# MLA softmax three items ahead of its transposes; state-space rows as one product, two buffers of decayed x, first merges later

## What is computed

```python
def block(args):                                   # MLA, 16 heads, blocks of 128 queries
    s = einsum('bqhd,bkhd->bhqk', qn, k_nope) + einsum('bqhr,bkr->bhqk', qr, k_rope)
    s = where(key_pos <= q_pos, s * scale, -inf)
    p = softmax(s, axis=-1)
    return einsum('bhqk,bkhv->bqhv', p, v)

def ssd_scan(xh, dt, a, bmat, cmat):               # chunks of 128, 4 groups of 8 heads
    x = xh * dt
    a_cum = cumsum(dt * a, axis=2)
    decay = exp(where(tri, a_cum[:, :, :, None] - a_cum[:, :, None, :], -inf))
    cb = einsum("bclgn,bcsgn->bclsg", cm, bm)
    y_diag = einsum("bclsgr,bcsgrp->bclgrp", cb[..., None] * decay, x)
    decay_states = exp(a_cum[:, :, -1:] - a_cum)
    states = einsum("bclgn,bclgrp->bcgrpn", bm, x * decay_states[..., None])
    # scan over chunks: h = h * exp(a_cum[:, :, -1]) + states
    y_off = einsum("bclgn,bcgrpn->bclgrp", cm, prev) * exp(a_cum)[..., None]
    return y_diag + y_off

merged = sigmoid(g_att) * y_att + sigmoid(g_ssm) * y_ssm
```

## Time and profile before

| | us |
|---|---|
| median of 3 runs | 2668.32 |
| lowest, highest | 2663.45, 2671.43 |
| profiled execution, device time | 2666.76 |
| its span in the profile | 2664.9 |
| TensorE busy in the span | 2557.8 (96%) |
| VectorE busy | 1531.3 (57%) |
| GpSimd busy | 1138.1 (43%) |
| ScalarE busy | 670.0 (25%) |
| mean granted TensorE clock | 0.988 |

### The profile page before, as it was taken

How to read it: one execution, slowest core, us unless ns; L and a number is a source line. 1 busy time by engine, 2 the same in 40 slices (tenths; PEclk the granted TensorE clock), 3 DMA queues, 4 the chain that set the end, 5 groups by cost and what they waited for, 6 DMA issues and landing times.

```text
span 2664.9 us, 31050 instructions
## 1 busy us (share of the span) xinstructions
PE 2557.8 (96%) x11716; PEld 2035.1 (76%) x11716; DVE 1531.3 (57%) x2061; ACT 670.0 (25%) x1315; POOL 1138.1 (43%) x765
## 2 busy tenths in 40 slices
PE   8999999999988999999999999999989998999998
PEld 6888888888766778888886677777766666788886
DVE  4764665464776533735556674444445787677721
ACT  2003520021444421201113213333322442222200
POOL 4333455555522135555553353333322224555554
PEclk9999999999999999999998999999999999999999
DMA  6334556665522236665664474454454435565665
GB/s 206 125 111 128 165 190 193 199 192 189 174 79 77 67 111 190 193 197 194 206 190 142 137 239 158 158 170 141 150 199 133 148 115 166 183 196 190 190 194 169
DMA packets 149562, 436.63 MB, mean 164 GB/s; under 512 B 14064, under 2 KB 18352, under 8 KB 149424
## 3 DMA queue, kind: packets, MB, share of 16 engines
q1 hardware_dynamic: 64480, 200.29, 25.6%
q0 software_dynamic: 67840, 201.35, 21.7%
q10 hardware_dynamic: 17104, 33.14, 3.6%
HBM read 417.90 MB, written 16.83 MB: 163 GB/s over the span
## 4 chain that ended last, share of the span: by engine, by line
PE 50%; POOL 18%; issue 17%; DVE 9%; DMA 2%; DVEq 2%; ACT 1%; POOLq 0%; ACTq 0%; SPq 0%
POOL w_lo L422 15%; PE bank L479 12%; PE bank L481 12%; PE bank L482 12%; POOL w_hi L394 4%; DMA projections<-spill_out 1%; PE bank L1127 1%; PE bank L1118 1%; DVE mla_probs L2188 1%; PE bank L950 1%; PE bank L684 1%; PE bank L937 1%; DVE rope_sum L2106 1%; DVE mla_probs L2405 1%; PE bank L1153 1%
## 5 line engine op out<-in xcount | busy, mean ns | idle before, releaser
L422 POOL TENSOR_TENSOR w_lo<-w_raw,w_hi 128x1024 fp32r<-128x1024 f32 x375 | 901.9, 2405 | 11.7 <-DMA w_hi<-stream 3.7
L394 POOL DMA_DIRECT2D w_hi<-stream x376 | 227.6, 605 | 1497.4 <-PE bank L479 1297.9
L479 PE MATMUL bank<-x_hi,w_hi 128*128 128x512 f32 x1464 | 588.3, 402 | 17.8 <-POOL w_lo L408 11.5
L481 PE MATMUL bank<-x_lo,w_hi 128*128 128x512 f32 x1464 | 573.7, 392 | 0.0
L482 PE MATMUL bank<-x_hi,w_lo 128*128 128x512 f32 x1464 | 573.4, 392 | 0.0
L479 PEld LDWEIGHTS bank<-x_hi,w_hi 128*128 128x128 f32 x1464 | 277.2, 189 | 101.2 <-issue 39.8
L482 PEld LDWEIGHTS bank<-x_hi,w_lo 128*128 128x128 f32 x1464 | 277.1, 189 | 59.0
L481 PEld LDWEIGHTS bank<-x_lo,w_hi 128*128 128x128 f32 x1464 | 277.4, 189 | 56.7 <-issue 2.5
L2053 DVE TENSOR_TENSOR relu_sq<-relu 128x512 f32<-128x512 f32 x64 | 181.8, 2840 | 97.7 <-ACT relu L1428 97.7
L479 PE MATMUL bank<-hidden_hi,w_hi 128*128 128x512 f32 x512 | 199.2, 389 | 0.0
L481 PE MATMUL bank<-hidden_lo,w_hi 128*128 128x512 f32 x512 | 199.2, 389 | 0.0
(11 more groups left out here) (441 smaller groups left out, 4536.1 us busy)
## 6 DMA issues: line engine op xcount, KB each, us to landing
w_hi<-stream POOLq DMA_DIRECT2D x376, 512.0 KB, 4.8
w_raw<-stream SPq DMA_DIRECT2D x376, 512.0 KB, 3.7
projections<-spill_out ACTq DMA_DIRECT2D x56, 256.0 KB, 2.1
ssm_x<-projections ACTq DMA_DIRECT2D x4, 1024.0 KB, 6.8
gate_tiles<-projections ACTq DMA_DIRECT2D x16, 256.0 KB, 2.9
ssm_z<-projections ACTq DMA_DIRECT2D x16, 256.0 KB, 2.6
residual<-x_in SPq DMA_DIRECT2D x4, 512.0 KB, 6.8
toeplitz_hi<-toeplitz_rows_hi POOLq DMA_DIRECT2D x4, 512.0 KB, 6.4
```

The lines of the kernel that those rows point to most:

```text
L394: e.dma_start(in_slot(whi, t % SLOTS, o), in_stream(o)).then_inc(hi_ready[t % SLOTS], 16)
L422: e.tensor_tensor(wlo[:, s, :], raw[:, s, :], whi[:, s, :].bitcast(F32), ALU.subtract).then_inc(lo_ready, 1)
L479: mm = e.matmul(out, wh, rh, start=first, stop=False)
L481: e.matmul(out, wh, rl, start=False, stop=False)
```

## The change

Four things change. In MLA the distance of 2 becomes `MLA_AHEAD = 3` in the loops of TensorE, ScalarE and VectorE; `mpr` keeps its three buffers, and the conditions of the waits stay. The high and low rows of the cumulative sums become one tile of 64 partitions (`sat_rows`), selected by a column of two identities above each other (`both`, which ScalarE writes in two copies), so that `rows` and `decay_rows` take one matmul where they took two. `ssm_xd` gets a second buffer: VectorE makes the first two decayed x at B and the third after S0. And VectorE merges a0, a1 and a2 after T3, S0 and S2 instead of T0, T3 and S1.

```diff
+MLA_AHEAD = 3
...
-        sah, sal = at("ssm_acum_t_hi", 198, [32, S], F32R), at("ssm_acum_t_lo", 202, [32, S], F32R)
+        sat_rows, both = at("ssm_acum_t", 198, [64, S], F32R), at("hi_and_lo_row", 207.5625, [64, 32], F32R)
+        sah, sal = sat_rows[0:32, :], sat_rows[32:64, :]
...
-        sxd, sbn = at("ssm_xd", 148, [P, S]), ...
+        sxd, sbn = [at(f"ssm_xd{x}", kb, [P, S]) for x, kb in enumerate((148, 202))], ...
...
-                for n in range(MLA_ITEMS + 2):
+                for n in range(MLA_ITEMS + MLA_AHEAD):
                     if n < MLA_ITEMS:
                         scores(n)
-                    m = n - 2
+                    m = n - MLA_AHEAD
...
-                        sel = identr[0:32, 2 * n + q:2 * n + q + 1].broadcast_to([32, P])
-                        e.matmul(o[:, :], sel, sah[:, :], start=True, stop=False)
-                        e.matmul(o[:, :], sel, sal[:, :], start=False, stop=False)
+                        sel = both[:, 2 * n + q:2 * n + q + 1].broadcast_to([64, P])
+                        e.matmul(o[:, :], sel, sat_rows[:, :], start=True, stop=False)
...
-                    e.matmul(bank[3][:, :], sel, sah[:, :], start=True, stop=False)
-                    e.matmul(bank[3][:, :], sel, sal[:, :], start=False, stop=True).then_inc(ea_full, 1)
+                    e.matmul(bank[3][:, :], sel, sat_rows[:, :], start=True, stop=True).then_inc(ea_full, 1)
...
-                    if n >= 6 and (n - 6) % 4 == 0:
-                        out_low((n - 6) // 4)
+                    done = n - MLA_AHEAD - 4
+                    if done >= 0 and done % 4 == 0:
+                        out_low(done // 4)
...
                     elif kind == "B":
                         decayed_x(g, 0)
+                        decayed_x(g, 1)
...
-                        if c < 2:
-                            decayed_x(g, c + 1)
+                        if c == 0:
+                            decayed_x(g, 2)
...
                 def decayed_x(g, c):
-                    e.drain()
+                    if c == 0:
+                        e.drain()
+                    if 3 * g + c >= 2:
+                        e.wait_ge(st_pe, 3 * g + c - 1)
...
-                    units("first", i)
+                    units("first", {3: 0, 5: 3, 7: 6}.get(i, -1))
```

More of the change, by code:

```diff
@@ L344, in build @@
         sst = [at(f"ssm_state{x}", 136 + 6 * x, [P, 3, S]) for x in range(2)]
-        sxd, sbn = at("ssm_xd", 148, [P, S]), [at(f"ssm_b_nat{x}", 150 + 2 * x, [P, ST, P]) for x in range(2)]
+        sxd, sbn = [at(f"ssm_xd{x}", kb, [P, S]) for x, kb in enumerate((148, 202))], [at(f"ssm_b_nat{x}", 150 + 2 * x, [P, ST, P]) for x in range(2)]
         sgt = [[at(f"ssm_g{p}{q}", 164 + 4 * p + 2 * q, [P, S]) for q in range(2)] for p in range(2)]
@@ L600, in build @@
         STEP_UNITS = []
-        for _s in range(MLA_ITEMS + 2):
+        for _s in range(MLA_ITEMS + MLA_AHEAD):
             _now = []
@@ L1230, in prep @@
                             e.wait_ge(e_bn, g + 1)
-                        e.matmul(bank[4][:, :], sbn[g % 2][:, c, :], sxd[:, :], start=True, stop=True).then_inc(st_pe, 1)
+                        e.matmul(bank[4][:, :], sbn[g % 2][:, c, :], sxd[(3 * g + c) % 2][:, :], start=True, stop=True).then_inc(st_pe, 1)
                 for i, task in enumerate(PREP):
@@ L1631, in projections @@
                         e.wait_ge(dt_pe, 1)
-                        e.activation(sah[:, :], bank[2][0:32, :], ACT.Copy).then_inc(dt_act, 1)
+                        for x in range(2):
+                            rows_ = slice(32 * x, 32 * x + 32)
+                            e.activation(both[rows_, :], identr[rows_, rows_].bitcast(F32), ACT.Copy)
+                        e.activation(sah, bank[2][0:32, :], ACT.Copy).then_inc(dt_act, 1)
             def sparse_attention():
@@ L1705, in exponentials @@
                         e.activation(ssel[:, :, :],
-                                     identr[0:32, 2 * n:2 * n + 8].bitcast(F32).unsqueeze(2).broadcast_to([32, 8, 64]), ACT.Copy)
+                                     both[:, 2 * n:2 * n + 8].bitcast(F32).unsqueeze(2).broadcast_to([64, 8, 64]), ACT.Copy)
                     e.wait_ge(sg_sel, n + 1)
@@ L2321, in time_sums @@
                 e.tensor_copy(sat[:, :, :], bank[1][:, 0:P].rearrange("p (c n) -> p c n", n=32))
-                tt(sal[:, :], bank[2][0:32, :], sah[:, :].bitcast(F32), ALU.subtract)
+                tt(sal, bank[2][0:32, :], sah.bitcast(F32), ALU.subtract)
                 e.drain()
```

4 lines of the change are left out of this document (2 added, 2 removed).

## The result

The changed kernel takes 2651.41 us (median of 7 runs, 2648.74 to 2655.71), the kernel before on the same chip 2671.43 (7 runs, 2662.40 to 2674.72). The ratio is 0.9935, 95% interval 0.9920 to 0.9951: 17.4 us faster by it (13 to 21 in the interval), 20.0 by the medians. The prediction had 32 us, and its range ended at 2649. The profiled execution's span is 2649.7 us against 2664.9.

What follows compares the result with a forecast made beforehand. The prediction took TensorE to bound both stages. MLA's 14.6 us and the state space's 17.6 summed to 32.2 us off the profiled execution's 2666.76, giving 2634.6, or 2636 as median; range 2625 to 2649.

Steps and rivals of the forecast that it cites:

- The 17.2 us of waits go: MLA: twelve waits of TensorE's transposes for VectorE's scaled probabilities, 17.2 us in all, disappear with one more item of distance.
- Nine ordinary heads pay 0.2 each: MLA: in nine heads the output product newly waits 0.2 us for ScalarE's copy, 1.8 us in all.
- Three rotary heads pay 1.2 each: MLA: in three heads with VectorE's rotary steps between, the output product waits 1.2 us each, 3.6 in all.
- an output product that waits over 1 us in a head with units: MLA: named beforehand as a sign that the prediction would be wrong.
- 4.0 us of clock back: MLA: of 8.6 us lost to TensorE's low clock, 4.0 are regained, bounds 0 and 5.
- Unit-less heads, period about 8.9, no gain: MLA: two heads without units take about 8.9 us between output products, 8.97 before; waits of 0.9 return, 1.8 in all.
- The tail, 10.25 to 8.9: MLA's end: from the last but one output product to the first product of `mla_o`, 10.25 us becomes 8.9.
- The first items: MLA's first six items stay bound by VectorE's rotary steps; the first output product comes some 0.7 us later.
- State space, start, 7.5 us: State-space start: unit a1 4.8 us earlier, clock 1.3, first state product's wait 0.6 and second's 0.8 less; 7.5 in all.
- 48 matmuls at 0.23: State-space head steps: 48 removed matmuls are worth 0.23 us each, 11.0 us, bounds 8 and 15.8.
- 0.9 us lost to waits: Head steps: longer waits for chunk copies take 1.2 us, the last state products' waits give 0.3; 11.0 becomes 10.1.
- The chain in all heads: Rival: each of 15 MLA heads pays 0.9 us or more, MLA gives 3 us, the whole 2648; chance 0.12.

Runs made afterwards that it cites:

- e5: The changed kernel with GpSimd's `w_lo` of three weight tiles filled with zeros instead of computed, leaving out part of four units; 2638.08 us, ratio 0.9884 to before.
- e2: The changed kernel with `MLA_AHEAD` back at 2, so only the state-space edits; 2655.80 us, ratio 0.9953 to the kernel before.
- e1: The kernel before with `MLA_AHEAD = 3` and its three uses, nothing else; 2666.05 us, ratio 0.9992 to the kernel before.
- e18: The changed kernel with MLA distance back at 2 and twelve `w_lo` held by waits for VectorE's scalings; 2637.38 us, ratio 0.9891 to before.
- e20: e18 with VectorE's state of the next group ahead of the merge in the p = 3 head steps; 2642.08 us, ratio 0.9888 to before.
- e9: The changed kernel with VectorE's state of the next group ahead of the merge in the p = 3 head steps; 2650.37 us, ratio 0.9932 to before.

## Why the prediction was wrong, point by point

**The 17.2 us of waits go**: right, 1.5 are left, under the 5 named. The scalings held by `w_lo` that it expected to stay are gone too: none in MLA lasts over 0.6 us after. **Nine ordinary heads pay 0.2 each**: they pay nothing.

**Three rotary heads pay 1.2 each: this is the step that failed.** They paid 3.5. Without the meeting of `w_lo` and `rope_sum` it is 0.85 (e5), so the order on ScalarE and VectorE was read rightly and GpSimd left out. The prediction named this as a sign of being wrong (an output product that waits over 1 us in a head with units), without a cause for it. The trace of before had it: a scaling held 2.83 us by `w_lo`, and a `rope_sum` only 0.7 us ahead of the next `w_lo`. I kept VectorE's durations and moved only TensorE. But the start of `w_lo` hangs on TensorE (it follows the first product out of a tile, 1.5 us behind it before and 1.4 after), and taking 1.8 us of waiting and the half clock behind it out of TensorE moved it 2.35 us against VectorE. 3 x 2.3 = 6.9 us of the missing 10.9.

**4.0 us of clock back**: nothing came back (0.95 over MLA after, 0.96 before; 0.98 or more was named), since each 3.5 us wait had its own low clock behind it. Counted as the prediction does, 10.2 us are lost to the clock against 8.5: the 4.0 and 1.7 more. With the 6.9, and less the 1.8 that the ordinary heads don't pay, this makes 10.8 of the 10.9. It follows from the same step: in e5 no low clock stands behind the three output products (6.0 us lost, at the first items and the tail).

**Unit-less heads, period about 8.9, no gain**: 8.8 measured; their product waits 0.4 and not 0.9. **The tail, 10.25 to 8.9**: 9.0. **The first items**: the first output product comes 1.2 us later, 0.7 predicted.

**State space, start, 7.5 us**: 6.0 in the profiled execution, 7.7 in e2, which has no low clock there. Piece by piece: a1 5.1 (4.8 predicted), chunks 1.44 apart (1.5), the first state product's wait down by 0.45 (0.6), the second's by 0.75 (0.8). Right.

**48 matmuls at 0.23**: right, three to a step make 0.70 in steps without waits. **0.9 us lost to waits**: mis-sized. Up to the last rows 45 of the matmuls are gone, 10.35 us, and e2, without a low clock, gains 8.4 (185.25 to 176.8): 1.9 lost. The transposes' waits for chunk copies grew by 1.8 (1.2 predicted); I had not listed the wait of `ssm_head_rows`' product for VectorE's `ssm_y`, which has its bank (1.1 us in two places, none before); the last state products' waits fell by 0.9 (0.3 predicted). In the last step that product waits another 1.4, and from its rows to the product that sums the squares of y it is 0.8 longer than before (19.7 us in e2 against 18.9), where 0.7 less was counted on: 3.4 lost of the 11.0 in all. In the profiled execution of after another 1.6 is clock.

**The rivals.** The chain in all heads (MLA 3 us, 2648) is near in time and wrong in mechanism: e1's and the full kernel's heads with units don't wait unless they are rotary. The measured 3.7 us of MLA has another cause.

The prediction drew on the Trainium skill (TensorEngine Tiling (Array Packing), Tiling Modes, Key Properties), which says that a change of the tiling mode drains TensorE. The runs agree as far as the time goes: it is 0.43 and 0.43 us between 64-row and 128-row products, and a removed matmul was worth 0.23 and not 0.33. That the added time is a drain no run here shows.

## What to carry to other kernels

When a wait of the bounding engine is taken away, everything that this engine releases (slots, and so the loads and conversions of a helper engine) starts earlier against the other engines: look at what runs on the third engine within the removed time, on both sides, and whether the two can hold each other. The work of an engine that is rarely waited for can be placed by a wait of its own, and here nine such waits were worth more (12 us by the ratio, 7 to 17 in its interval) than another item of distance (2, 0 to 5); the place has a latest point too, the next reader of what it makes. Cutting its work into pieces without a gap between them made both kernels slower here. And a stage of one profiled execution can differ by 4 us from another of the same code by the clock alone (e18 and e20): compare waits first.

## What was not expected of the hardware

VectorE got no turn between four GpSimd instructions that followed each other directly, 0.70 us apart: `rope_sum` took 4.87 us beside 2.81 of them. A GpSimd fill that writes the same tile held it not at all (2.07). The instruction that is held can start first in the rows: the scaling starts at 763.97 and `w_lo` at 764.21, `y_lo` in e9 at 2182.25 and `w_lo` at 2182.64. Which of two is held can't be read from the order of their starts.

The granted clock fell in one execution and stayed at 1.00 in another at the same place with the same waits (0.88 us before the second state product): 26.8 against 25.1 us for the start of the state space. Of thirteen profiled executions with this code six had the low clock there. What decides that is open; a gain or loss of 1.6 us there says nothing of an edit.
